# Sums of squares in the gated-delta part: one 4-byte product of ones against two single-pass products of a rounded and a remaining part

## The reference, cut to what matters

```python
def l2norm(x):
    return x * lax.rsqrt(jnp.sum(x * x, axis=-1, keepdims=True) + EPS)
q = jnp.repeat(l2norm(q.reshape(Bn, T, N_QK_HEADS, HEAD_K)), rep, axis=2)
...
o, S = gated_delta_rule(q, k, v, g, beta, s_gdn.astype(jnp.float32))
o = rmsnorm(o, gdn_norm) * jax.nn.silu(z...)      # rmsnorm: x * rsqrt(mean(x * x) + EPS) * gain
```

## Time and profile before

| | |
|---|---|
| time, median of 3 | 2583.14 us (2583.01 to 2584.31) |
| profiled execution, its own time | 2588.41 us |
| its span, first to last instruction | 2586.7 us |
| PE busy | 2546.2 us (98%) |
| weight loads of PE busy | 2525.4 us (98%) |
| DVE busy | 1662.3 us (64%) |
| ACT busy | 1321.6 us (51%) |
| POOL busy | 510.2 us (20%) |
| mean granted TensorE clock | 0.992 of 2.4 GHz |
| chain that ended last | PE 92% |

### The profile page before, as it was taken

One profiled execution on the slowest core, in us unless ns is written; L12 is line 12 of the kernel. 1 busy time (PEld: TensorE's weight loads), 2 busy tenths in 40 slices (PEclk: granted clock), 3 DMA queues, 4 the chain that ended last, 5 costly groups with the idle time before them and its releaser, 6 DMA issues.

```text
span 2586.7 us, 50475 instructions
## 1 busy us (share of the span) xinstructions
PE 2546.2 (98%) x20848; PEld 2525.4 (98%) x20848; DVE 1662.3 (64%) x2862; ACT 1321.6 (51%) x2013; POOL 510.2 (20%) x912
## 2 busy tenths in 40 slices
PE   8999999999999999999999999999999999999997
PEld 7999999999999999999999999999999999999997
DVE  5767777686777765433365566566776656776665
ACT  6545646464655644333244344445665545665664
POOL 1527163452716340000000000200110000110100
PEclk8999999999999999999999999999999999999999
DMA  7656565555656556677755566757986768986563
GB/s 210 180 146 192 144 174 154 160 167 155 183 147 176 152 164 196 177 211 213 205 167 180 179 200 200 242 178 250 320 277 216 220 189 254 311 283 189 167 204 116
DMA packets 445718, 507.38 MB, mean 196 GB/s; under 512 B 21329, under 2 KB 423914, under 8 KB 443066
## 3 DMA queue, kind: packets, MB, share of 16 engines
q1 hardware_dynamic: 417072, 415.43, 53.1%
q0 software_dynamic: 27840, 88.53, 11.3%
q10 hardware_dynamic: 578, 0.19, 0.0%
HBM read 478.16 MB, written 26.49 MB: 195 GB/s over the span
## 4 chain that ended last, share of the span: by engine, by line
PE 92%; DVE 2%; DMA 2%; POOL 1%; ACT 1%; issue 1%; DVEq 0%; POOLq 0%; ACTq 0%
PE bank L700 91%; DMA raw<-in_w_ffn_down 1%; DVE wlo L1364 1%; POOL sol L555 1%; POOL prod L552 1%; ACT whi L1033 1%; DMA raw<-in_w_ple_gate 0%; PE bank L791 0%; PE bank L780 0%; DMA blk<-blk_scratch 0%; ACT sqr L1272 0%; DMA DT<-sol_scratch 0%; DVE xlo L1404 0%; ACT xhi L1332 0%; PE bank L724 0%
## 5 line engine op out<-in xcount | busy, mean ns | idle before, releaser
L700 PE MATMUL bank<-xhi,whi 128*128 128x264 f32 x5520 | 1591.9, 288 | 7.2 <-DVE wlo L1364 4.2
L700 PE MATMUL bank<-xlo,whi 128*128 128x264 f32 x5520 | 1569.0, 284 | 0.0
L700 PE MATMUL bank<-xhi,wlo 128*128 128x264 f32 x5520 | 1566.5, 284 | 0.0
L1364 DVE TENSOR_TENSOR wlo<-raw,whi 128x1024 fp32r<-128x1024 f32 x828 | 1013.5, 1231 | 727.6 <-ACT whi L1033 726.9
L1033 ACT ACTIVATE whi<-raw 128x1024 fp32r<-128x1024 f32 x828 | 872.5, 1057 | 810.9 <-PE bank L700 743.6
L700 PEld LDWEIGHTS bank<-xhi,whi 128*128 128x128 f32 x5520 | 1041.8, 189 | 10.3 <-issue 6.6
L700 PEld LDWEIGHTS bank<-xlo,whi 128*128 128x128 f32 x5520 | 1042.5, 189 | 2.0 <-issue 1.9
L700 PEld LDWEIGHTS bank<-xhi,wlo 128*128 128x128 f32 x5520 | 1039.3, 188 | 0.0
L700 PE MATMUL bank<-ahi,whi 128*128 128x264 f32 x704 | 200.1, 284 | 2.5 <-DVE wlo L1364 2.5
L700 PE MATMUL bank<-ahi,wlo 128*128 128x264 f32 x704 | 200.1, 284 | 0.0
L700 PE MATMUL bank<-alo,whi 128*128 128x264 f32 x704 | 199.7, 284 | 0.0
(11 more groups left out here) (306 smaller groups left out, 1827.4 us busy)
## 6 DMA issues: line engine op xcount, KB each, us to landing
raw<-in_w_in SPq DMA_DIRECT2D x356, 512.0 KB, 4.1
raw<-in_w_ffn_gate SPq DMA_DIRECT2D x88, 512.0 KB, 5.2
raw<-in_w_ffn_up SPq DMA_DIRECT2D x88, 512.0 KB, 4.7
raw<-in_w_ffn_down SPq DMA_DIRECT2D x96, 384.0 KB, 3.5
raw<-in_w_gdn_out SPq DMA_DIRECT2D x64, 512.0 KB, 3.5
chunkS<-in_state_gdn POOLq DMA_DIRECT2D x16, 1024.0 KB, 7.4
raw<-in_w_sconv_out SPq DMA_DIRECT2D x32, 512.0 KB, 3.5
raw<-in_w_o SPq DMA_DIRECT2D x32, 512.0 KB, 4.4
```

The lines of the kernel that those rows point to most:

```text
L700: return pe.matmul(out, lhsT, rhs, start=start, stop=stop)
L1364: dve.tensor_tensor(wlo[:, at_ % SPLIT, :, :], raw[:, at_ % RAW, :, :], f32(whi[:, at_ % SPLIT, :, :]), ALU.subtract).then_inc(lo_ready, 1)
```

## The change

Two tiles of type float32r are laid over other tiles: `sq_hi` over `sv` (where `cs` lies too), and the remainders `q_lo` over QK and `o_lo` over PT. The ones become a float32r tile; other users see the same bytes as float32. The squares are now formed twice on ACT, once rounded into `sq_hi` and once in full; DVE subtracts one from the other (two new steps, `qlo` at 11 and `olo` at 7), and PE adds two float32r products in place of each float32 product. The semaphores `qsq` and `osq` now count two per group. `qsum` moves from step 11 to 12, `qroot` from 12 to 13, `qn` from 13 to 14; `qk` stays at 15.

```diff
-    ones = new("ones", [P, P])
+    ones_r = new("ones_r", [P, P], F32R)
+    ones = ones_r[:, :].bitcast(F32)
...
+    sq_hi = at("sq_hi", [P, NCH, 4 * CH], F32R, sv_at)
+    o_lo = at("o_lo", [P, NCH, 4 * CH], F32R, pt_at)
+    q_lo = at("q_lo", [P, NCH, 4 * CH], F32R, qk_at)
...
-        PE_STEP = {"cur": {5: ("kk",), 10: ("nturn",), 11: ("qsum",), 15: ("qk",), ...
+        PE_STEP = {"cur": {5: ("kk",), 10: ("nturn",), 12: ("qsum",), 15: ("qk",), ...
-        ACT_STEP = {"cur": {1: ("exps",), 5: ("kcopy",), 10: ("qsq",), 11: ("ncopy",), 12: ("qroot",),
+        ACT_STEP = {"cur": {1: ("exps",), 5: ("kcopy",), 10: ("qsq",), 11: ("ncopy",), 13: ("qroot",),
-        DVE_STEP = {"cur": {5: ("lt",), 13: ("qn",), 16: ("qkt",), ...
+        DVE_STEP = {"cur": {5: ("lt",), 11: ("qlo",), 14: ("qn",), 16: ("qkt",), ...
-                    "prev": {0: ("r",), 2: ("e1",), 4: ("u1",), 6: ("s2",), 9: ("o",)},
+                    "prev": {0: ("r",), 2: ("e1",), 4: ("u1",), 6: ("s2",), 7: ("olo",), 9: ("o",)},
...
                 elif slot == "qsum":
-                    pe.wait_ge(g["qsq"], gr + 1)
+                    pe.wait_ge(g["qsq"], 2 * gr + 2)
                     if gr > 0:
                         pe.wait_ge(g["olog"], gr)
-                    mm(B[4][:, :], ones[:, :], QK[:, 1, :]).then_inc(g["qsum"], 1)
+                    mm(B[4][:, :], ones_r[:, :], sq_hi[:, 0, :], True, False)
+                    mm(B[4][:, :], ones_r[:, :], q_lo[:, 1, :], False, True).then_inc(g["qsum"], 1)
                 elif slot == "osum":
-                    pe.wait_ge(g["osq"], gr + 1)
+                    pe.wait_ge(g["osq"], 2 * gr + 2)
                     pe.wait_ge(g["s2"], gr + 1)
-                    mm(B[4][:, :], ones[:, :], PT[:, 0, :])
-                    mm(B[7][:, :], ones[:, :], PT[:, 1, :]).then_inc(g["osum"], 1)
+                    for c in range(NCH):
+                        mm(B[4 + 3 * c][:, :], ones_r[:, :], sq_hi[:, c, :], True, False)
+                        m = mm(B[4 + 3 * c][:, :], ones_r[:, :], o_lo[:, c, :], False, True)
+                    m.then_inc(g["osum"], 1)
...
                 if slot == "qsq":
                     act.wait_ge(silu_done, 4 * gr + 2)
+                    act.activation(sq_hi[:, 0, :].rearrange("p (b t) -> p b t", b=2), sqk[:, 0:2, 0:T], ACT.Square)
                     act.activation(QK[:, 1, :]..., ACT.Square).then_inc(g["qsq"], 1)
                 elif slot == "o0c":
                     act.activation(vTok[:, 0, :, :]..., bank[6][:, :], ACT.Copy)
+                    act.activation(sq_hi[:, 0, :], bank[6][:, :], ACT.Square)
                     act.activation(PT[:, 0, :], bank[6][:, :], ACT.Square)
                 elif slot == "osq":
                     act.activation(vTok[:, 1, :, :]..., bank[7][:, :], ACT.Copy)
+                    act.activation(sq_hi[:, 1, :], bank[7][:, :], ACT.Square)
                     act.activation(PT[:, 1, :], bank[7][:, :], ACT.Square).then_inc(g["osq"], 1)
...
+                elif slot == "qlo":
+                    dve.wait_ge(g["qsq"], 2 * gr + 1)
+                    dve.tensor_tensor(q_lo[:, 1, :], QK[:, 1, :], f32(sq_hi[:, 0, :]), ALU.subtract).then_inc(g["qsq"], 1)
+                elif slot == "olo":
+                    dve.wait_ge(g["osq"], 2 * gr + 1)
+                    dve.tensor_tensor(o_lo[:, :, :], PT[:, :, :], f32(sq_hi[:, :, :]), ALU.subtract).then_inc(g["osq"], 1)
```

More of the change, by code:

```diff
@@ L153, in trunk @@
     Tt = new("Tt", [P, NCH, 4 * CH])
+    qk_at = top[0]
     QK = new("QK", [P, NCH, 4 * CH])
     Nn = new("Nn", [P, NCH, 4 * CH])
+    pt_at = top[0]
     PT = new("PT", [P, NCH, 4 * CH])
@@ L419, in freed_all @@
                 eng.wait_ge(pair_free[m % 2], m // 2 + 1)
-        PE_STEP = {"cur": {5: ("kk",), 10: ("nturn",), 11: ("qsum",), 15: ("qk",), 18: ("tails",), 19: ("vturn",),
+        PE_STEP = {"cur": {5: ("kk",), 10: ("nturn",), 12: ("qsum",), 15: ("qk",), 18: ("tails",), 19: ("vturn",),
                            27: ("pt",), 28: ("pt0",), 29: ("pe0",), 30: ("pf0",), 31: ("s1",)},
@@ L429, in trunk @@
                     "first": {6: ("kcopy",), 7: ("exps",)}}
-        DVE_STEP = {"cur": {5: ("lt",), 13: ("qn",), 16: ("qkt",), 27: ("mask",), 28: ("e0",),
+        DVE_STEP = {"cur": {5: ("lt",), 11: ("qlo",), 14: ("qn",), 16: ("qkt",), 27: ("mask",), 28: ("e0",),
                             29: ("ktok",), 30: ("u0",), 31: ("next_exponents",)},
-                    "prev": {0: ("r",), 2: ("e1",), 4: ("u1",), 6: ("s2",), 9: ("o",)},
+                    "prev": {0: ("r",), 2: ("e1",), 4: ("u1",), 6: ("s2",), 7: ("olo",), 9: ("o",)},
                     "first": {6: ("exponents",), 7: ("lt",)}}
@@ L496, in _ @@
             mine.inc(pool.memset(ident[:, :], 0.0))
-            mine.inc(pool.memset(ones[:, :], 1.0))
+            mine.inc(pool.memset(ones_r[:, :].bitcast(F32), 1.0))
             mine.inc(pool.memset(eps[:, :], EPS))
```

## The result

The changed kernel takes 2610.93 us (median of 4, 2610.62 to 2614.02) against 2583.35 before: ratio 1.0109, 95% interval 1.0091 to 1.0126. It is slower by 27.6 us; forecast were 2604.5, +21.4. Profiled execution against profiled execution it is 2614.02 against 2588.41, spans 2612.3 against 2586.7, +25.6.

A forecast was written before the change was run, and what follows sets the result against it. PE, busy 98% of the span, was taken to set the pace. Terms -10.1 + 7.4 + 19.6 + 4.5 gave +21.4 us on the median 2583.14: 2604.5 us, range 2593 to 2614.

The forecast's parts named there:

- products cheaper: PE's `qsum` and `osum`: float32r products in place of float32 save 1.26 us per group, 10.1 us in all.
- wait for `olo`: PE before `osum`: stands still 0.93 us per group because `olo` follows the remainder of piece 10 on DVE; 7.4 us.
- wait for `qn`, groups 1 to 7: PE before `qk`: idle 2.45 us per group, as `qn` follows the remainder of piece 17, copied after the SiLU.
- wait for `qn`, group 0: The same PE wait before `qk` in the start-up group: taken at 2.45 us, may differ by a microsecond.
- falls of the clock: PE's clock halves after some idle times before `qk`: three falls at 1.5 us, 4.5 us; bounds 0 and 12.
- wait for DT in group 0 gone, with its fall: PE's single 3.77 us wait in group 0 of the kernel before; the prediction's sum had no term for its going.
- the forecast's own 2600 to 2606: Whole kernel: PE waits for both `olo` and `qn`, with zero to four clock falls; 60%.
- The four shares of the clock: PE's granted shares 0.60, 0.50, 0.50, 0.70 in one earlier fall of 3.4 us, used to price a fall.
- `qk` does not wait: Rival at PE's `qk`: `qn` is ready in time, sum -2.7 us, 2580.4, no measurable change; 8%.
- the reserve of 2.9 us: Before `qk` in the old order: `qn` was finished that much before PE was ready for `qk`.
- The chain keeps inside the piece: Rival at `osum` and `qk`: ACT and DVE finish in time, PE sees only cheaper products; -10.1 us, 2573.0; 7%.
- The clock falls at every wait: Rival at PE's eight waits for `qn`: the clock falls each time, +28.9 us, 2612; 15%.

The follow-up runs named there:

- experiment 3: Changed kernel with `qn` back at step 13 and `olo` at step 6 on DVE: 2575.73 us against 2582.0 for the kernel before, ratio 0.997.
- experiment 2: Changed kernel with `olo` alone moved, to step 6 on DVE, ahead of the remainder of piece 10: 2600.72 us, ratio 1.0074 to the kernel before.
- experiment 1: Changed kernel with `qn` alone moved back to step 13 on DVE: 2582.91 us, ratio 1.0006 to the kernel before.
- experiment 6: Changed kernel with ACT's SiLU of v0 one step later, behind the copy of piece 17, `qn` still at 14: 2585.79 us, ratio 1.0013 to the kernel before.
- experiment 5: Kernel before, float32 products kept, with only `qsum`, `qroot` and `qn` moved to steps 12, 13 and 14: 2605.91 us, ratio 1.0088.

## Why the prediction was right

**The steps in order.** Terms of the sum, as forecast and as the runs give them (profiled executions, in us):

| term | forecast | measured | from |
|---|---|---|---|
| products cheaper | -10.1 | -9.5 | 1.19 x 8 (experiment 3) |
| wait for `olo` | +7.4 | +9.0 | 1.17 x 6 (experiment 2), 0.2 less in the last two |
| wait for `qn`, groups 1 to 7 | +17.2 | +18.3 | 115.78 - 113.17 = 2.61, x 7 |
| wait for `qn`, group 0 | +2.4 | +4.3 | idle 4.06, restart as in the others |
| falls of the clock | +4.5 | +7.6 | five at 1.53 (118.48 - 116.95) |
| wait for DT in group 0 gone, with its fall | 0 | -5.5 | 3.77 idle; 1.7 for the fall, an estimate from the earlier trace rows |
| sum | +21.4 | +24.2 | spans: +25.6 |

Up to the end of the last `osum` (993.64 before, 1017.67 after) the two executions differ by 24.0. The other 1.6 arise behind it, where the change moved nothing: two waits for remainders were 1.38 and 1.14 before and are 1.90 and 2.46 now, and the traces of the experiments have 0.5 to 1.8 in the same places.

The time lies inside the range of 2593 to 2614 but above the forecast's own 2600 to 2606. The mechanism was right in each term that was named; what was off are sizes, and one term was missing. (1) A wait costs more than its idle time. PE's idle time before `osum` is 0.89, the period loses 1.17; before `qk` 2.35 against 2.61. After a standstill the first products are spaced wider (0.33 in place of 0.23, the block of `qk` 1.16 in place of 1.05), and the idle time is counted from the modelled end of the last product, which lies 0.16 behind the pitch. I had counted a start 0.14 after the release and a full pitch from there. `olo` itself, which I had taken at the 1.23 of the remainder, took 1.42 in six of eight groups. (2) Group 0 waits 4.06; I had seen that it lies in the start-up and left it at 2.45. (3) Five falls in place of three. (4) The term that I did not have is the DT wait of group 0, which the new waits cover; by the estimate above the profiled executions would differ by some 31 without it, in place of 25.6.

**Luck.** The named terms came to 29.7 against 21.4, 8.3 too little; the missing term gave 5.5 of it back by the profile's number. Without it the time would have come out at about 2616, above the range. The 5.3 us by which I brought the profiled time down to the median was 3.1 for the changed kernel. That the time lies in the range rests in part on two errors that cancel.

**Two slips in the working.** 2.45 is as near to 2.10 (0.35) as to 2.81 (0.36), so the argument for the rival that the clock falls every time had no weight. With half of 1.23 off, the lower bound of the wait for `olo` is 0.3, not 0.4. Neither moves the sum. The four shares of the clock that the working quotes are right; the one from 143 to 144, which the earlier trace rows leave out:

```profile
143.00:144.00 1.00, 1.00 (x7) 1.00 (x7) 0.63 (x2) 0.00 (x0) 1.00 (x3) 0.50 0.04 6
```

**The bounds.** The single-pass product of 512 columns was bounded by 0.215 and 0.235 from two rows and came out at 0.23, at the scaled end. The sustained pace of 131 ns that the Trainium skill gives for this size (TensorE: Matmul & The Clock Gate, section "Back-to-back issue gap") does not hold here; the trace has 0.23.

**The rivals.** "`qk` does not wait" is what experiment 1 makes of it, and experiment 6 nearly: the reserve of 2.9 us was true of the old order. "The chain keeps inside the piece" is experiment 3, with the places changed. "The clock falls at every wait" did not occur; five of eight is between it and the forecast, and by my own division (from five falls on) the case was that rival's.

**Cover.** The three squares were costed at nothing behind the idle times of the earlier trace rows, `qlo` at nothing. Experiment 3 confirms this for the period: it has the products' saving and nothing else.

**What is open.** The medians differ by 27.6, the spans of the profiled executions by 25.6. The kernel before has its profiled time 5.3 above its median, the changed one 3.1. In the traces of the experiments the DT wait of group 0 is 0, 1.1, 1.7 or 3.2 us, so a part of the 2 us may be that the profile of before caught a long one; no trace of its timed runs shows it.

## What to carry to other kernels

Where engines work through fixed lists, ask for the place of an addition before you ask for its length: here a subtraction of 1.2 to 1.4 us cost 1.17 per group behind a remainder that waits for the bottleneck engine, and nothing one step earlier. Before a step is moved, look at what stands directly ahead of it on each engine and what that waits for; `qn` needed nothing of piece 17 and lost 2.6 us to it. When a cheaper instruction makes the kernel slower, run the reordering alone, without the cheaper instruction: it gave nearly the whole loss here.

## What the runs showed of the hardware

The same idle time of TensorE (2.35 us, or 2.0) brought the granted clock down to 0.50 in some groups and left it at 1.00 in others of the same execution. After 2.35 it fell in groups 1, 3, 5 and 7 of the changed kernel and not in 2, 4 and 6; after 2.0, in experiment 5, in groups 4 and 7 and not in 1, 2, 3, 5 and 6. So the length of the idle time alone does not decide it at these lengths; what does is open. A fall cost 1.4 to 1.6 us where one period can be set against another (118.48 against 116.95; 117.38 and 117.16 against 115.78 in experiment 2). Filling the idle time with products whose result nobody reads kept the clock up from 72 to 1060 us of the profiled execution.

The first product after a wait started 0.05 us behind the end of the `olo` or `qn` that released it (0.14 at 84.13 in the kernel before), and a wait cost 0.26 to 0.28 us more than the idle time that the profile lists; 0.07 us of idle time before `qk` still cost 0.33 per group (experiment 6).
